# The opening of a hybrid DeltaNet and RG-LRU layer: nine x buffers, staggered steps, and the gate third of the modulation moved to the last scan

## The reference

```python
xs = x_sample + grid_pos_embed(...)          # halves: by grid row (16), by column (64)
mod_ctx = jax.nn.silu(c_ctx[None]) @ ada_w + ada_b      # ada_w: 1024 x 3072
mod_lat = jax.nn.silu(c) @ ada_w + ada_b
shift, scale, gate = jnp.split(mod, 3, axis=-1)
h = rmsnorm(x, pre_w) * (1 + scale) + shift
proj = h @ w_in                                # q, k, v, z, b, a, rx, rgate
o_dn, s_dn = delta_branch(...)                 # 8 heads, two directions, chunks
o_rg, s_rg = rglru_branch(...)                 # 8 blocks, two directions
y = jnp.concatenate([o_dn, o_rg], -1) @ w_out
return x + gate * rmsnorm(y, post_w), s_dn, s_rg
```

## Time and profile before

| | us |
|---|---|
| median of 3 runs | 1524.68 |
| lowest, highest | 1523.77, 1526.91 |
| the profiled execution | 1524.72 |
| its span | 1523.1 |
| mean granted clock of TensorE | 0.96 |

### The profile page before, as it was taken

One profiled execution on the slowest core, in us unless ns is written; L12 is line 12 of the kernel. 1 busy time (PEld: TensorE's weight loads), 2 busy tenths in 40 slices (PEclk: granted clock), 3 DMA queues, 4 the chain that ended last, 5 costly groups with the idle time before them and its releaser, 6 DMA issues.

```text
span 1523.1 us, 24595 instructions
## 1 busy us (share of the span) xinstructions
PE 1391.1 (91%) x8182; PEld 1248.2 (82%) x8182; DVE 1027.9 (67%) x2135; ACT 753.3 (49%) x1912; POOL 115.3 (8%) x135
## 2 busy tenths in 40 slices
PE   5966899999999989999999999899989997599997
PEld 1266898899799879988997998799889976388886
DVE  3565477779677877887797778778877966722222
ACT  2351357564646465565647464745666484511111
POOL 0000100010001000100000010001000000212211
PEclk9978999999799999999999999999999998699999
DMA  8702111110111211111111111102111150523440
GB/s 306 249 14 68 28 29 32 57 44 30 40 49 44 57 48 28 60 33 42 44 44 36 53 44 49 55 22 67 33 42 45 44 225 20 153 77 110 124 123 29
DMA packets 95235, 102.79 MB, mean 67 GB/s; under 512 B 4230, under 2 KB 81271, under 8 KB 94089
## 3 DMA queue, kind: packets, MB, share of 16 engines
q1 hardware_dynamic: 92170, 90.70, 19.4%
q0 software_dynamic: 2944, 10.49, 1.8%
HBM read 85.88 MB, written 15.29 MB: 66 GB/s over the span
## 4 chain that ended last, share of the span: by engine, by line
PE 77%; ACT 8%; DVE 6%; issue 5%; DMA 3%; SPq 0%; DVEq 0%; ACTq 0%
PE bank L673 14%; PE bank L675 14%; PE bank L674 14%; PE bank L947 12%; PE bank L901 2%; PE bank L868 2%; PE bank L784 2%; PE bank L909 2%; PE bank L917 2%; PE bank L894 2%; PE bank L889 2%; PE bank L824 2%; DMA arena<-pos_row 2%; PE bank L746 1%; ACT L1089 1%
## 5 line engine op out<-in xcount | busy, mean ns | idle before, releaser
L673 PE MATMUL bank<-hT_hi,w_hi 128*128 128x384 f32 (+1 forms) x1224 | 442.0, 361 | 30.9 <-DVE w_lo L1379 17.6
L675 PE MATMUL bank<-hT_hi,w_lo 128*128 128x384 f32 (+1 forms) x1224 | 419.4, 343 | 0.0
L674 PE MATMUL bank<-hT_lo,w_hi 128*128 128x384 f32 (+1 forms) x1224 | 419.4, 343 | 0.0
L673 PEld LDWEIGHTS bank<-hT_hi,w_hi 128*128 128x128 f32 x1224 | 235.8, 193 | 33.7 <-DVE w_lo L1379 18.5
L674 PEld LDWEIGHTS bank<-hT_lo,w_hi 128*128 128x128 f32 x1224 | 235.9, 193 | 1.2
L675 PEld LDWEIGHTS bank<-hT_hi,w_lo 128*128 128x128 f32 x1224 | 234.9, 192 | 0.0
L1225 ACT ACTIVATE arena<-bank,arena 128x128 f32<-128x128 f32 x272 | 78.7, 369 | 176.2 <-PE bank L901 176.0
L1469 DVE SCALAR_TENSOR_TENSOR arena<-arena 128x1154 f32<-128x1154 f32 x96 | 137.5, 1433 | 3.5 <-DVE arena L1467 1.1
L947 PE MATMUL bank<-wo_hi,ot_hi 128*128 128x512 f32 x288 | 114.3, 397 | 18.8 <-DVE ot_lo L1758 13.5
L947 PE MATMUL bank<-wo_lo,ot_hi 128*128 128x512 f32 x288 | 113.6, 395 | 0.0
L947 PE MATMUL bank<-wo_hi,ot_lo 128*128 128x512 f32 x288 | 113.3, 393 | 0.0
(11 more groups left out here) (224 smaller groups left out, 2388.4 us busy)
## 6 DMA issues: line engine op xcount, KB each, us to landing
w_raw<-w_in SPq DMA_DIRECT2D x51, 512.0 KB, 4.0
arena<-ada_w SPq DMA_DIRECT2D x8, 1536.0 KB, 10.8
arena<-scr_G SPq DMA_DIRECT2D x16, 576.0 KB, 4.8
ot<-scr_o SPq DMA_DIRECT2D x9, 1024.0 KB, 6.7
arena<-x_sample SPq DMA_DIRECT2D x16, 512.0 KB, 7.3
wo<-w_out SPq DMA_DIRECT2D x4, 2048.0 KB, 16.0
scr_o<-arena POOLq DMA_DIRECT2D x8, 576.0 KB, 4.2
arena<-pos_row SPq DMA_DIRECT2D x32, 128.0 KB, 5.5
```

The source lines that it names most:

```text
L673: pe.matmul(out, w_hi[:, slot, k], hT_hi[:, k, cols], start=first, stop=False)
L674: pe.matmul(out, w_hi[:, slot, k], hT_lo[:, k, cols], start=False, stop=False)
L675: return pe.matmul(out, w_lo[:, slot, k], hT_hi[:, k, cols], start=False, stop=last)
```

## The change

- Nine x buffers. All of x is loaded at once, with no wait for a buffer. Positions are loaded once: 16 rows of 512 and 64 rows twice. PE puts the row half into a bank with a product by `row_pick` (a one-hot matrix that DVE makes), DVE adds it from there; POOL adds the column half.
- Staggered steps. Step `i` adds tile `i`, takes the mean of tile `i-1`, scales tile `i-2` and copies tile `i-3`; turned blocks go to four banks, with one copy of 512 columns on DVE and one on ACT in place of four each.
- `ada_w` is loaded with its first 2048 columns, six blocks, then the `ba` weights, two blocks, then tile k. Its products (four a block) go to partitions 0, 32, 64 and 96 of bank 0.
- `ada_b` comes in turned with the other small rows and is added to the turned columns; DVE and ACT copy two rows each.
- Modulation goes by the three column groups. PE waits for `hT_lo` block by block, and projects ba(0), k(0), ba(1), ba(2), k(1), turns `ba`, and projects k(2).
- The convolutions of k and q move on DVE ahead of the running sums and ahead of the wait for `scr_G`; the high parts of tiles move on ACT to match.
- Gate third. SP loads it (4 MB) ahead of `w_out` in the last head; PE makes 16 products of 2 by 512 in the last scan, two in each step from 1 to 8; DVE adds them to `ada_b`'s row behind the last `mean_o`; `scr_gate` is stored then.

```diff
+            sp.dma_start(x_in[:, 0], x_prompt[0]).then_inc(x_loaded[0], 16)
+            sp.dma_start(pos_row_in, pos_row).then_inc(pos_in, 16)
+            for half in range(2):
+                sp.dma_start(pos_col_in[64 * half:64 * half + 64, :], pos_col).then_inc(pos_in, 16)
+            for t in range(1, NCH):
+                sp.dma_start(x_in[:, t], x_sample[0, P * (t - 1):P * t, :]).then_inc(x_loaded[t], 16)
+
...
+                sp.dma_start(adaw[:, k, :], ada_w[0, k * P:(k + 1) * P, 0:2 * D]).then_inc(ada_in[k], 16)
+
+            for k in range(6):
+                load_ada(k)
+            load_w(1, w_in2[:, OFF_B:OFF_B + P].rearrange("(k p) n -> p k n", p=P))
+            load_ada(6)
+            load_ada(7)
+            load_w(0, w_tile("k", 0))
...
+            sp.wait_ge(silu_c_made, 1)
+            sp.dma_start(scr_c, silu_c.rearrange("p s k -> p (s k)")).then_inc(silu_c_stored, 16)
...
-            load_x(1, x_in, pos, 0, x_loaded)
-            load_ada(0)
-            for b in range(2):
-                for half in range(2):
-                    sp.dma_start(pos[64 * half:64 * half + 64, b, 512:], pos_col).then_inc(pos_in, 16)
-            load_ada(1)
...
-            for t in range(2, NCH):
-                sp.wait_ge(x_turned, 2 * t - 2)
-                load_x(t % 2, x_in, pos, t - 1, x_loaded)
-                if t + 1 < KT:
-                    load_ada(t + 1)
-            def load_w(slot, src):
-                sp.dma_start(w_raw[:, slot], src).then_inc(w_loaded[slot].sem, 16)
-
-            sp.wait_ge(x_squared, NCH)
-            load_w(1, w_in2[:, OFF_B:OFF_B + P].rearrange("(k p) n -> p k n", p=P))
...
+            sp.wait_ge(proj_taken.sem, proj_taken.prev(h, 12))
+            sp.wait_ge(silu_c_stored, 16)
+            sp.dma_start(silu_c_late.rearrange("p s k -> p (s k)"), scr_c).then_inc(gate_in, 16)
+            sp.dma_start(gate_row, ada_b[0:1, 2 * D:].to_broadcast([2, D])).then_inc(gate_in, 16)
+            for q in range(2):
+                sp.dma_start(adaw_gate[:, 4 * q:4 * q + 4, :],
+                             ada_w[0, 512 * q:512 * q + 512, 2 * D:].rearrange("(k p) n -> p k n", p=P)).then_inc(gate_in, 16)
             for q in range(4):
                 sp.dma_start(wo[:, 4 * q:4 * q + 4, :],
                              w_out2[512 * q:512 * q + 512, :].rearrange("(k p) n -> p k n", p=P)).then_inc(w_out_in[q], 16)
+            sp.wait_ge(gate_row_made, 2)
+            sp.dma_start(scr_gate, gate_row).then_inc(gate_stored, 16)
...
+            gp.wait_ge(pos_in, 48)
+            for n in range(1, NCH):
+                gp.wait_ge(x_loaded[n], 16)
+                gp.tensor_tensor(x_in[:, n, 512:], x_in[:, n, 512:], pos_col_in, ALU.add).then_inc(pos_col_added, 1)
...
+            def put_pos_row(n):
+                if n >= 3:
+                    pe.wait_ge(x_added, n - 2)
+                pe.matmul(banks[1 + n % 2][:, :], row_pick[:, P * (n - 1):P * n], pos_row_in, start=True, stop=True)\
+                  .then_inc(pos_row_put, 1)
+
...
-                if n < KT:
-                    pe.wait_ge(ada_in[n], 16)
-                    for j in range(6):
-                        mm = pe.matmul(banks[j][0:2, :], silu_c[:, :, n], adaw[:, n, 512 * j:512 * j + 512],
-                                       start=(n == 0), stop=(n == KT - 1))
-                        if n == KT - 1:
-                            mm.then_inc(ada_done, 1)
...
-            for m in range(16):
-                pe.wait_ge(mod_row_made, m // 4 + 1)
-                mm = pe.transpose(banks[6][:, 2 * m:2 * m + 2], mod_row[0:2, P * m:P * m + P], ident[0:2, 0:2])
-            mm.then_inc(mod_turned, 1)
-            pe.wait_ge(mod_row_made, 6)
...
+                pe.wait_ge(ada_in[k], 16)
+                for j in range(4):
+                    mm = pe.matmul(banks[0][32 * j:32 * j + 2, :], silu_c[:, :, k], adaw[:, k, 512 * j:512 * j + 512],
+                                   start=(k == 0), stop=(k == KT - 1))
+                    if k == KT - 1:
+                        mm.then_inc(ada_done, 1)
...
+            pe.wait_ge(row_pick_made, 1)
+            pe.wait_ge(pos_in, 48)
+            put_pos_row(1)
+            pe.wait_ge(silu_c_made, 1)
+            for i in range(1, NCH + 2):
+                if i + 1 < NCH:
+                    put_pos_row(i + 1)
+                if i >= 2:
+                    turn_x(i - 2)
+                if i >= 5:
+                    ada_rows(i - 5)
+            for k in range(NCH - 3, KT):
+                ada_rows(k)
+            for j in range(4):
+                pe.wait_ge(mod_row_made_v if j < 2 else mod_row_made_a, j % 2 + 1)
+                if j == 3:
+                    pe.wait_ge(h_made_v, NCH)
...
+            pe.wait_ge(w_lo_made.sem, 1)
+            project_ba(0)
+            pe.wait_ge(w_lo_made.sem, 2)
+            project_k(0)
+            project_ba(1)
+            project_ba(2)
+            project_k(1)
             pe.wait_ge(baT_made, 3)
             for ch in range(NCH):
                 mm = pe.transpose(banks[2][:, 32 * ch:32 * ch + 32], baT[0:32, col(ch):col(ch) + P], ident[0:32, 0:32])
             mm.then_inc(ba_turned, 1)
+            project_k(2)
...
+                    mm = pe.matmul(banks[half][0:2, :], silu_c_late[:, :, k], adaw_gate[:, k, 512 * half:512 * half + 512],
+                                   start=(k == 0), stop=(k == KT - 1))
...
+                        mm.then_inc(gate_done, 1)
+
                 pe.wait_ge(dZ_taken.sem, dZ_taken.at(b, 30))
+                if last:
+                    pe.wait_ge(gate_in, 16 * 4)
+                    pe.wait_ge(gate_tanh.sem, gate_tanh.at(b, 12))
...
+                        if last:
+                            gate_product(step - 1, 0)
...
+                    if last and step:
+                        gate_product(step - 1, 1)
...
+            for i in range(NCH + 3):
+                if i < NCH:
+                    if i == 0:
+                        act.wait_ge(x_loaded[0], 16)
+                    else:
+                        act.wait_ge(x_added, i)
+                        act.wait_ge(pos_col_added, i)
+                        act.wait_ge(x_squared, i)
+                    act.activation(square_out, x_in[:, i], ACT.Square, accum_out=x_ss[:, i:i + 1]).then_inc(x_squared, 1)
...
+            high_w(1, 16)
+            for j in (2, 3):
+                act.wait_ge(ada_done, j + 1)
+                r = slice(32 * j, 32 * j + 2)
+                act.activation(mod_row[r, :], banks[0][r, :], ACT.Copy).then_inc(mod_row_made_a, 1)
...
+                    high_h(g, k)
+                    if k + MOD_V < KT:
+                        modulate(g, k + MOD_V)
+                if g == 0:
+                    high_w(0, 16)
...
-            act.wait_ge(raw_cleared, 1)
-            for n in range(3):
-                take_first(n)
+            act.wait_ge(raw_cleared, 2)
+            take_first(0)
+            take_first(1)
+            high_w(1, 32)
...
-            high_w(1, 32)
-            for n in range(3, 6):
-                take_first(n)
+            take_first(2)
+            take_first(3)
+            high_w(0, 32)
+            take_first(4)
+            take_first(5)
...
+            act.activation(kT, RA, ACT.Silu, scale=2.0).then_inc(silued.sem, 1)
             high_w(1, 48)
...
+            for i in range(NCH + 3):
+                if 1 <= i < NCH:
+                    dve.wait_ge(x_loaded[i], 16)
+                    dve.wait_ge(pos_row_put, i)
+                    dve.tensor_tensor(x_in[:, i, 0:512], x_in[:, i, 0:512], banks[1 + i % 2][:, :], ALU.add).then_inc(x_added, 1)
+                if 1 <= i <= NCH:
+                    dve.wait_ge(x_squared, i)
+                    dve.tensor_scalar(x_ss[:, i - 1:i], x_ss[:, i - 1:i], 1.0 / D, EPS, ALU.mult, ALU.add).then_inc(x_meaned, 1)
...
+                    dve.wait_ge(x_rooted, n + 1)
+                    own(dve.reciprocal(x_ss[:, n:n + 1], x_ss[:, n:n + 1]))
+                    dve.tensor_scalar(x_in[:, n], x_in[:, n], x_ss[:, n:n + 1], None, ALU.mult).then_inc(x_normed, 1)
...
+            def low_h(g, k):
+                o, w = GROUPS[g]
+                dve.wait_ge(h_hi_made, KT * g + k + 1)
...
+            for g in range(len(GROUPS)):
+                for k in range(MOD_V - 2):
+                    modulate(g, k)
                 for k in range(KT):
-                    dve.wait_ge(h_hi_made, KT * n + k + 2)
-                    dve.tensor_tensor(hT_lo[:, k, o:o + w], hT[:, k, o:o + w], hT_hi[:, k, o:o + w].bitcast(F32),
-                                      ALU.subtract).then_inc(h_lo_made, 1)
-                if n == 0:
-                    low_w(1, 1)
-            low_w(0, 2)
+                    low_h(g, k)
+                    if k < 2:
+                        modulate(g, MOD_V - 2 + k)
+                if g == 0:
+                    low_w(0, 2)
...
+            conv_first(0, RA)
+            low_w(0, 4)
...
```

(8 more changed lines are left out.)

294 lines of the change are left out of this document (138 added, 156 removed).

## The result

The changed kernel takes 1478.5 us in the median of its first four runs (1474.1 to 1494.5), beside 1525.8 for the kernel before on the same chip: a ratio of 0.969, interval 0.962 to 0.977. The forecast was 1476, the range 1463 to 1492. Two single executions of later kernels, 1954.8 us in position_k128 and 2246.1 us in both_and_gate_post_late, came with a granted clock of 0.65 and 0.55 over the whole span and stand outside the times given here.

What follows compares the result with a forecast made beforehand. Opening taken as bound by DMA, then DVE, then a chain between engines until phase_a; PE bounds phase_a and is the longest part of a last-scan step. 1524.7 - 58.0 + 9.5 = 1476.2, forecast 1476 us, range 1463 to 1492.

Steps and rivals of the forecast that it cites:

- Bytes: Opening loads: 13.9 MB up to the last ada block, at 363 GB/s 38.3 us, landed at 45.7 us.
- Rival D: Opening: loads don't come as a full stream, last block lands 12 us later, 1488 us; chance 0.04.
- Quarters: Opening on PE: four products in four column quarters take 2.1 us a set, between bounds 0.89 and 3.54.
- Rival A: Opening: the quarters run one after the other, PE 11.3 us later, 1488 us; chance 0.16.
- Modulation: Between opening and projections: starts at 51.1 us, 2.9 behind the products; PE begins 2.4 later, at 53.5, 36.0 earlier.
- First tiles: First projection product to phase_a: 74.0 us instead of 96.1, since the waits for w_lo (17.6 us) go.
- C: First tiles: DVE later than its 5 us cover, PE waits 3 to 8 us and loses clock, 1482; chance 0.08.
- E: First tiles: clock stays at the lower level, 360 products cost 53.3 us more, 1529.5, slower; chance 0.02.
- Stretch to phase_a: Everything ahead of phase_a: it begins at 127.5 us instead of 185.5, 58.0 us gained.
- Last scan: Sixteen gate products in the last scan: 1.3 us in a normal step, 9.5 us more in all.
- Rival B: Last scan hides more of the gate products, costing 3 us, 1470 us; chance 0.10.
- phase_a and the rest: From phase_a on, apart from the last scan's products: stays bound by PE, loads and additions hide, 0 us.

Runs made afterwards that it cites:

- position_k128: Changed kernel with the opening's position product over 128 rows instead of 16, the table's rows loaded eight times: 1483.4 us, ratio 0.971.
- both_and_gate_post_late: Changed kernel with gate products in quarters behind the scan, 128-row position products, and GpSimd's gate rows waiting for wo's sixteenth low half: 1462.2 us, ratio 0.958.
- second profile: Profile of the unedited changed kernel run once more, in four more runs: span 1474.9 us; those runs 1477.5 us, ratio 0.969.
- first profile: Profile of the changed kernel's longest run among its first four, 1494.5 us: span 1492.9 us.
- quarters_behind_scan: Changed kernel with the gate third's products moved behind the last scan, as eight sets of four 256-column products on column quarters: 1457.3 us, ratio 0.957.

## Why the prediction was right

The number, 1476, is right for the reasons given in its large terms: less to load, no waits for w_lo, and sixteen products in the scan's path. But inside the opening and inside the last scan two wrong terms each cancelled, and that they did so to 0.1 and 0.6 us is luck.

- **Bytes.** Last ada block forecast at 45.7, landed at 44.2 and 44.4; the rate was 400 and 403 GB/s from 12 to 44 us, above the 363 of the earlier trace rows. Rival D is out: the DMA share stays at 0.99 or above from 16 to 44 us.
- **Quarters: term mis-sized.** Taken at 2.1 us a set, measured 0.97 at full clock (1.04 first start to last end), the near bound of 0.89 and a little. The argument "the next product's first pass lies beside the second pass of the one before" was wrong: all four products lie side by side. Rival A is out. The Trainium skill (TensorEngine Tiling (Array Packing), Overview) has a speedup of up to four for columns of 32 or fewer; the sets here reach 3.7 (3.54 / 0.97), so the page was nearer than my price. The drain that its section on Tiling Modes names shows as about 0.1 us a change.
- **Clock in the opening: a term left out.** Products and turns were priced at the upper level throughout. TensorE ran at the lower one until 34.6 or 45.8 us. I had taken the 1.00 of the earlier trace rows as full clock, and that column doesn't show the level ahead of its first change; the first set of six before, 8.12 us at 16 us where the earlier trace rows has 5.31, would have told. TensorE came to its first quarter product at 32.4 us instead of 24.1, 8.3 later, and needed 15.8 us from there instead of 24.1, 8.3 less. So the two errors cancel when the rate rises at 35 us (last quarter product 48.27, forecast 48.2), by luck, and leave 5.4 us when it rises at 46. The mechanism is settled by position_k128: products over 16 rows held the rate down.
- **Modulation.** Forecast 2.9 us from the last product to the first block; measured 2.5 (48.27 to 50.77), and 2.45 from there to PE: 2.4 was forecast.
- **First tiles.** Forecast 74.0, measured 73.5 in both profiles, and no wait for w_lo. Of its small terms, the waits for low parts of h were 0.3 us behind the first product, not 2.4, and the lower clock lasted 5.3 us, not 4. The experiment shows the cause as predicted for the largest wait: order on VectorE, 9.1 us of wait and 2.7 of clock. Rivals C and E are out.
- **Stretch to phase_a.** Forecast 58.0; 58.8 in the second profile, 53.4 in the first.
- **GpSimd in the opening.** 2.16 us for an addition was the price in the output stage, beside VectorE's work; eight took 10.8, 1.35 each, and hid.
- **Last scan.** Forecast 9.5; 8.9 in the second profile, 10.8 in the first, 10.9 by leaving the products out, 9.0 by moving them. Rival B is out. A normal step costs 1.7 us, not 1.3: the second product hides no more than the 0.2 us for which PE was idle. What is given back is larger than forecast: the fifth step, with its wait of 1.88 us and the lower clock behind it, became 0.8 us shorter. That the second profile lies at 8.9 and not at 10.8 is chance: TensorE was back at the upper level 3.2 us into that scan, ahead of the first gate product, against 8.5 us in the first profile and 8.7 before.
- **phase_a and the rest.** 0 forecast. Behind the scan 0.5 us less, from phase_a's turns to the last scan 1072.8 us in both.

What the prediction did not see is what the output stage had to give: 6.8 us by a wait on GpSimd. The stage is as long in the kernel before, 236.1 us, so the same is to be expected there, but no run shows it; the earlier trace rows had the mark of it, an addition of 2.16 us on GpSimd where the same form takes 1.27 alone.

## What to carry to other kernels

Price the clock from durations, not from the column: take an instruction whose time is known at both levels and look it up in each stretch; and where products that fill few rows make up much of TensorE's work, do not take the upper level for granted because TensorE is busy. Where an engine has a gap behind another's chain, independent products belong there and not into the steps of a recurrence: the same sums cost 9 to 11 us in the scan and nothing behind it. And where two engines that take turns both feed TensorE, the one whose result is due later should wait, even if it then starts 9 us later.

## What the hardware showed that I had not expected

- Narrow products side by side: four products of 128x2 by 128x512 in four column quarters of one bank took 0.97 us at the upper level ahead of turns and 0.86 in a row, where one alone takes 0.89; with 256 columns, 32 products took 3.64 us.
- TensorE, busy without a gap, stayed at its lower level for 27 us (19.1 to 45.8), while products over 16 rows took 2.07 of each 3.9 us (of each 5.7 from 32.7 us on); the same sequence over 128 rows had the upper level at 20 us. When it rises differs from run to run in the first case (33 to 46 us), and did not in the second (three profiles).
- VectorE and GpSimd took turns instruction by instruction where both read such tiles: a 128x1024 subtraction 1.14 us alone, 3.4 beside a 128x1024 multiplication, 2.3 beside a 128x512 addition; the multiplications 2.37 us alone, 3.2 and 3.3 beside it, and once 7.45 in quarters_behind_scan, where VectorE went first for five subtractions; additions of 128x512 1.27 alone and 2.2 beside.
- Open: which of the joins of the seven heads run at a lower clock in a run. Their work is the same each time, and no edit here touched it; it moves the kernel by up to 19 us between profiles, more than most edits.
